# A hybrid decoder layer on eight cores: transposes moved from TensorE to SyncE's DMA queue, eight buffers for the first loads, weight blocks cut in quarters

## The reference, cut to what matters

```python
a = rmsnorm(h, g_mix)
q, k, v, r, alow, u, vg = split_cols(a @ w_in, IN_SIZES)
# gated linear attention, S_t = diag(exp(log_a_t)) S_{t-1} + k_t^T v_t ; o_t = q_t S_t, per head
o, s_new = gla_recurrence(q, k, v, log_sigmoid(alow @ w_a2 + b_a) / 16, s0)
o = rmsnorm(o, g_gla_norm) * silu(r)
# spatial gate in chunks of 128 positions
vn = layernorm(gelu(vg), g_gmlp_ln, b_gmlp_ln)
m = rmsnorm(chunk_spatial_gate(gelu(u), vn, w_s, b_s), g_gmlp_out)
h = h + concatenate([o, m], axis=-1) @ w_out
f = rmsnorm(h, g_ffn)
gate, up = split_cols(f @ w_ffn_in, (5632, 5632))
h = h + (silu(gate) * up) @ w_ffn_out
h = h + rmsnorm(p_l @ w_ple, g_ple) * sigmoid(rmsnorm(h, g_ple_gate) @ w_ple_gate)
y = rmsnorm(h, g_final)
```

## Time and profile before

| | us |
|---|---|
| median of 3 runs | 1927.8 (1926.95 to 2220.32) |
| the profiled execution | 1927.42 |
| its span, slowest core | 1926.0 (cores: 1919.8 to 1926.0) |
| TensorE busy with matmuls | 1799.0 |
| VectorE, ScalarE, GpSimd busy | 785.6, 530.1, 117.6 |

### The profile page before, as it was taken

How to read it: one execution, slowest core, us unless ns; L and a number is a source line. 1 busy time by engine, 2 the same in 40 slices (tenths; PEclk the granted TensorE clock), 3 DMA queues, 4 the chain that set the end, 5 groups by cost and what they waited for, 6 DMA issues and landing times.

```text
span 1926.0 us, 27025 instructions; the slowest of 8 cores (1919.8 to 1926.0 us)
## 1 busy us (share of the span) xinstructions
PE 1799.0 (93%) x10124; PEld 953.7 (50%) x10124; DVE 785.6 (41%) x1242; ACT 530.1 (28%) x899; POOL 117.6 (6%) x133
## 2 busy tenths in 40 slices
PE   3888879989999999999999999999999999998996
PEld 2345434444444456655555656565656555544442
DVE  5545512461274351141515151515151515186666
ACT  4545413463471141000000000010100000026786
POOL 1001112120110000000000000000000000000000
PEclk9889989999999999999999999999999999999998
DMA  8930283506645524424242424334342434244212
GB/s 223 214 112 34 99 186 110 110 12 137 142 98 154 84 46 91 88 45 88 44 88 44 88 50 83 61 71 72 61 87 50 84 58 77 50 104 90 70 49 110
DMA packets 26198, 171.56 MB, mean 89 GB/s; under 512 B 3156, under 2 KB 4564, under 8 KB 13144
## 3 DMA queue, kind: packets, MB, share of 16 engines
q0 software_dynamic: 13248, 108.94, 32.3%
q1 hardware_dynamic: 12816, 60.90, 9.0%
q10 hardware_dynamic: 8, 0.01, 0.0%
HBM read 259.90 MB, written 18.87 MB: 145 GB/s over the span
## 4 chain that ended last, share of the span: by engine, by line
PE 80%; DMA 6%; DVE 5%; ACT 5%; issue 4%; DVEq 0%; ACTq 0%; POOL 0%; POOLq 0%; SPq 0%
PE pf L483 79%; ACT arena L445 3%; DVE arena L455 2%; DVE arena L463 1%; DMA arena<-xp 1%; DMA arena<-w_pg 1%; PE pb L493 1%; DMA arena<-xm 1%; DMA sso<-arena 1%; DMA arena<-st 1%; ACT L476 1%; ACT L445 1%; DMA arena<-w_al 1%; DVE arena L727 1%; DVE arena L452 0%
## 5 line engine op out<-in xcount | busy, mean ns | idle before, releaser
L483 PE MATMUL pf<-arena 128*128 128x384 bf16 (+4 forms) x9352 | 1754.2, 352 | 78.3 <-ACT arena L449 16.4
L483 PEld LDWEIGHTS pf<-arena 128*128 128x128 bf16 (+1 forms) x9352 | 904.3, 99 | 905.9 <-issue 117.6
L455 DVE TENSOR_TENSOR arena<-pf,arena 128x512 f32<-128x512 f32 (+3 forms) x641 | 419.4, 661 | 844.6 <-PE pf L483 774.9
L445 ACT ACTIVATE arena<-pf 128x384 bf16<-128x384 f32 (+4 forms) x310 | 159.2, 526 | 997.7 <-PE pf L483 980.6
L445 ACT ACTIVATE arena<-arena 128x512 f32<-128x512 f32 (+7 forms) x131 | 144.3, 1108 | 149.9 <-DVE arena L455 86.7
L455 DVE TENSOR_TENSOR arena<-arena 128x512 f32<-128x512 f32 (+6 forms) x139 | 101.1, 744 | 57.3 <-ACT arena L445 23.6
L463 DVE SCALAR_TENSOR_TENSOR arena<-arena 128x2048 bf16<-128x2048 f32 (+3 forms) x67 | 118.2, 1775 | 5.0 <-DVE arena L478 1.2
L449 ACT COPY arena<-pb 128x1024 bf16<-128x1024 bf16 x71 | 69.8, 1001 | 94.9 <-PE pb L493 94.8
L493 PE MATMUL pb<-arena 128*128 128x128 bf16 x772 | 60.3, 231 | 33.6 <-ACT arena L449 9.5
L184 POOL DMA_DIRECT2D arena<-w_f x55 | 29.0, 528 | 1018.7 <-PE pf L483 1015.8
L459 POOL TENSOR_TENSOR arena<-arena 128x1024 f32<-128x1024 f32 x30 | 66.3, 2213 | 356.3 <-ACT arena L449 226.4
(11 more groups left out here) (27 smaller groups left out, 88.8 us busy)
## 6 DMA issues: line engine op xcount, KB each, us to landing
arena<-w_f POOLq DMA_DIRECT2D x44, 1024.0 KB, 10.1
arena<-w_f POOLq DMA_DIRECT2D x11, 2048.0 KB, 14.7
arena<-xm SPq DMA_DIRECT2D x18, 1024.0 KB, 8.0
arena<-w_tok POOLq DMA_DIRECT2D x8, 2048.0 KB, 18.4
y<-arena SPq DMA_DIRECT2D x18, 512.0 KB, 2.8
arena<-xp SPq DMA_DIRECT2D x8, 1024.0 KB, 13.5
arena<-st SPq DMA_DIRECT2D x16, 512.0 KB, 4.6
sso<-arena SPq DMA_DIRECT2D x16, 512.0 KB, 2.9
```

The source lines that it names most:

```text
L445: S.op("act", lambda: nc.scalar.activation(out=out, in_=in_, func=func, **kw), reads=reads, writes=writes, cost=c_act(n, ptr) + (0.17 if " ...
L455: S.op("dve", lambda: nc.vector.tensor_tensor(out=out, in0=a, in1=b, op=op), reads=reads, writes=writes, cost=c_dve(n, rate))
L483: ins = nc.tensor.matmul(o, lhsT=l, rhs=r, start=st, stop=sp_)
```

## The change

1. `S.dmaT` is new: a DMA on SP with `transpose=True`, from SBUF to SBUF. It takes the place of the TensorE transposes and of the copies out of `pb` for the keys (`ktok`, eight of 128x512 to 128x4x128), the attention result (`catO`, nine of 128x1024), the spatial gate's result (`catM`, nine), the feed-forward norm (18) and the gate's norm (18): 54 of 128x1024 and eight of 128x512. The first norms of `xp` and `xm`, the keys of the first half and the sample keys stay on TensorE.
2. The eight `xp` tiles get eight buffers: two in `MI`, and two each in `RING[3]`, `RING[1]` and `RING[2]`. The `xm` loads cycle through the first four of them (before: two). So `w_tok` for the values waits for the buffers in rings 1 and 2, and `w_q` for the last use of those in ring 3. `g_mix` is loaded by one DMA on SP; a square root of a small tile (`pcol`) is issued at the start.
3. The weight blocks lie in HBM in quarters (`w_f1` in halves): 2048 values of a partition are contiguous, where 8192 were (`w_f1`: 4096). One DMA still loads the whole block.
4. The scheduler's constants: `DMA_RATE` 3.2e5 instead of 3.9e5, and `DMA_T`, 4.0, as the cost of a transposing DMA.

```diff
-DMA_RATE = 3.9e5
+DMA_RATE = 3.2e5
+DMA_T = 4.0
...
+    def dmaT(self, out, in_, reads=(), writes=(), boost=0.0):
+        nb = 2.0 * in_.shape[0] * in_.shape[1]
+        prev = self._touch(list(reads) + list(writes))
+        self.pend.append(Op("dma", "sp", (out, in_, True), list(reads), list(writes), writes[0], DMA_T, prev, nb, boost + self.bst))
...
+        if len(o.fn) == 3:
+            self.eng[e].dma_start(out=o.fn[0], in_=o.fn[1], transpose=True).then_inc(kb.dsem, 16)
...
-    w_tok = din("w_tok", [8, 128, 16, 512])
+    w_tok = din("w_tok", [8, 4, 128, 2048])
...
-            S.dma("pool", t, src, writes=[b], key=ring_key[i], after=after)
+            S.dma("pool", t.rearrange("p (q k) n -> p q (k n)", q=4), src.rearrange("q p n -> p q n"), writes=[b],
+                  key=ring_key[i], after=after)
...
-        for i in range(4):
-            t_, r_ = (MI if i < 2 else RING[3]).T([128, D], F32)
+        for i in range(8):
+            t_, r_ = (MI, RING[3], RING[1], RING[2])[i // 2].T([128, D], F32)
...
-        for n_ in range(4):
-            px.append(xload(xp, porder[n_], 4))
+        for n_ in range(8):
+            px.append(xload(xp, porder[n_], 8, 5000.0 - n_))
...
-        Wk, BWk = win_ch(0, w_k, "k", [[px[2][1]], [px[2][1]], [px[3][1]], [px[3][1]]])
+        Wk, BWk = win_ch(0, w_k, "k", [[px[1][1]], [px[3][1]], [px[5][1]], [px[6][1]]])
...
-                x_, Bx_ = xload(xm, t, 2)
+                x_, Bx_ = xload(xm, t, 4)
...
-                for tp in range(2):
-                    t0 = 4 * g + 2 * tp
-                    trans_to([kT[:, c, (t0 + u) * 128:(t0 + u + 1) * 128] for u in range(2) for c in range(4)], BkT[g],
-                             ktok[:, t0:t0 + 2, :], [Bktok[t0 // 2]], "act", 1024)
+                for c in range(4):
+                    S.dmaT(ktok[:, 4 * g:4 * g + 4, c * 128:(c + 1) * 128], kT[:, c, c0:c0 + n], [BkT[g][c]], [Bktok[4 * g + c]])
...
-            trans_to([on[i][:, j * 128:(j + 1) * 128] for j in range(8)], [Bon[i]], catO[:, t, :, :], [BcatO[t]], "act", 1024)
+            S.dmaT(catO[:, t, :, :], on[i], [Bon[i]], [BcatO[t]])
...
-            trans_to([mn[mi][:, j * 128:(j + 1) * 128] for j in range(8)], [Bmn[mi]], catM[:, t, :, :], [BcatM[t]] + Bgu[t], "act", 1024)
+            S.dmaT(catM[:, t, :, :], mn[mi], [Bmn[mi]], [BcatM[t]] + Bgu[t])
...
-            norm_p2(xf[t % 2], [Bxf[t % 2]], lambda hf: (catO if hf == 0 else catM)[:, t, :, :], Bf[t])
+            for hf in range(2):
+                S.dmaT((catO, catM)[hf][:, t, :, :], xf[t % 2][:, hf * 1024:(hf + 1) * 1024], [Bxf[t % 2]], [Bf[t][hf]])
...
-            norm_p2(xg[t % 2], [Bxg[t % 2]], lambda hf: (catO if hf == 0 else catM)[:, t, :, :], Bf[t], ("act", "act"))
+            for hf in range(2):
+                S.dmaT((catO, catM)[hf][:, t, :, :], xg[t % 2][:, hf * 1024:(hf + 1) * 1024], [Bxg[t % 2]], [Bf[t][hf]])
```

More of the change, by code:

```diff
@@ L183, in _emit @@
         kb.dcnt += 16
-        self.eng[e].dma_start(out=o.fn[0], in_=o.fn[1]).then_inc(kb.dsem, 16)
+        if len(o.fn) == 3:
+            self.eng[e].dma_start(out=o.fn[0], in_=o.fn[1], transpose=True).then_inc(kb.dsem, 16)
+        else:
+            self.eng[e].dma_start(out=o.fn[0], in_=o.fn[1]).then_inc(kb.dsem, 16)
         self._commit((kb.dsem, kb.dcnt), o.reads, o.writes)
@@ L389, in build_nc @@
     g_gout = din("g_gout", [1024])
-    w_out = din("w_out", [4, 128, 16, 512])
+    w_out = din("w_out", [4, 4, 128, 2048])
     g_ffn = din("g_ffn", [D])
-    w_f1 = din("w_f1", [2 * NFB, 2, 128, 16, 256])
-    w_f2 = din("w_f2", [NFB, 128, 4, D])
-    w_ple = din("w_ple", [128, 2, D])
+    w_f1 = din("w_f1", [2 * NFB, 2, 2, 128, 2048])
+    w_f2 = din("w_f2", [NFB, 4, 128, D])
+    w_ple = din("w_ple", [2, 128, D])
     g_ple = din("g_ple", [D])
     g_pg = din("g_pg", [D])
-    w_pg = din("w_pg", [4, 128, 16, 512])
+    w_pg = din("w_pg", [4, 4, 128, 2048])
     g_fin = din("g_fin", [D])
@@ L606, in build_nc @@
         dset(cm[:, :, 8:10], Bcm[3], 0.0)
+        S.op("dve", lambda: nc.vector.memset(pcol, 1.0), writes=[Bpcol], cost=0.1, boost=5000.0)
         def norm_p1(src, Bsrc, gain, Bg, xn, Bxn, ss, Bss):
@@ L733, in build_nc @@
         porder = [4, 5, 6, 7, 0, 1, 2, 3]
-        for c in range(4):
-            S.dma("act", grow[32 * c:32 * c + 1, :], g_mix[c * 512:(c + 1) * 512].unsqueeze(0), writes=[Bgrow[c]], boost=5000.0 - c)
+        S.dma("sp", grow[0:128:32, :], g_mix.rearrange("(c n) -> c n", c=4), writes=[Bgrow], boost=9000.0)
         px = []
-        for n_ in range(4):
-            px.append(xload(xp, porder[n_], 4))
+        for n_ in range(8):
+            px.append(xload(xp, porder[n_], 8, 5000.0 - n_))
             if n_ == 1:
-                S.dma("sp", wa2b, w_a2b, writes=Bwa2)
-        Wk, BWk = win_ch(0, w_k, "k", [[px[2][1]], [px[2][1]], [px[3][1]], [px[3][1]]])
+                S.dma("sp", wa2b, w_a2b, writes=Bwa2, boost=4998.5)
+        S.op("act", lambda: nc.scalar.activation(out=pcol[:, 0:1], in_=pcol[:, 0:1], func=AF.Sqrt, bias=EPS, scale=1.0), reads=[Bpcol],
+             writes=[Bpcol], cost=1.5, boost=5000.0)
+        Wk, BWk = win_ch(0, w_k, "k", [[px[1][1]], [px[3][1]], [px[5][1]], [px[6][1]]])
         bg_ = [nextpf() for _ in range(4)]
         MM([(bg_[c][0][:], onerow[32 * c:32 * c + 1, :], grow[32 * c:32 * c + 1, :], True, True) for c in range(4)],
-           [Bonerow] + Bgrow, [x[1] for x in bg_], 2.0)
+           [Bonerow, Bgrow], [x[1] for x in bg_], 2.0)
         for c in range(4):
@@ L795, in build_nc @@
             prev_norm(n_)
-        for n_ in range(4, 8):
-            px.append(xload(xp, porder[n_], 4))
         d1 = prev_decay(1)
@@ L856, in build_nc @@
         ktok, r_ = MI.T([128, 8, 512], BF16)
-        Bktok = S.bufs(4, "ktok", [part(r_, 2048 * i, 2048) for i in range(4)])
+        Bktok = S.bufs(8, "ktok", [r_] * 8)
         kTs, r_ = MI.T([128, 4, 128], BF16)
@@ L1488 @@
     blocks = lambda w, n: np.ascontiguousarray(w.reshape(16, 128, -1, n).transpose(2, 1, 0, 3))
+    quart = lambda w: np.ascontiguousarray(w.reshape(4, 4, 128, -1, 512).transpose(3, 0, 2, 1, 4)).reshape(-1, 4, 128, 2048)
     wa2b = np.zeros((128, 128), np.float32)
@@ L1492 @@
         wa2b[32 * c + 16] = f(b_a).reshape(512)[c * 128:(c + 1) * 128]
-    wf1 = f(w_ffn_in).reshape(16, 128, 2, 2 * NFB, 256)
+    wf1 = f(w_ffn_in).reshape(2, 8, 128, 2, 2 * NFB, 256)
     shared = {
         "g_mix": f(g_mix).reshape(D), "w_q": blocks(win[:, 0:512], 128), "w_k": blocks(win[:, 512:1024], 128),
-        "w_tok": blocks(np.concatenate([win[:, 1024:3072], win[:, 3088:5136]], axis=1), 512),
+        "w_tok": quart(np.concatenate([win[:, 1024:3072], win[:, 3088:5136]], axis=1)),
         "w_al": np.ascontiguousarray(win[:, 3072:3088].reshape(16, 128, 16).transpose(1, 0, 2)),
@@ L1500 @@
         "b_sT": np.ascontiguousarray(np.concatenate([bsT, np.tile(bsT[0:8], (16, 1))], axis=1)),
-        "g_gout": f(g_gmlp_out).reshape(1024), "w_out": blocks(f(w_out).reshape(D, D), 512), "g_ffn": f(g_ffn).reshape(D),
-        "w_f1": np.ascontiguousarray(wf1.transpose(3, 2, 1, 0, 4)),
-        "w_f2": np.ascontiguousarray(f(w_ffn_out).reshape(NFB, 4, 128, D).transpose(0, 2, 1, 3)),
-        "w_ple": np.ascontiguousarray(f(w_ple).reshape(2, 128, D).transpose(1, 0, 2)),
-        "g_ple": f(g_ple).reshape(D), "g_pg": f(g_ple_gate).reshape(D), "w_pg": blocks(f(w_ple_gate).reshape(D, D), 512),
+        "g_gout": f(g_gmlp_out).reshape(1024), "w_out": quart(f(w_out).reshape(D, D)), "g_ffn": f(g_ffn).reshape(D),
+        "w_f1": np.ascontiguousarray(wf1.transpose(4, 3, 0, 2, 1, 5)).reshape(2 * NFB, 2, 2, 128, 2048),
+        "w_f2": f(w_ffn_out).reshape(NFB, 4, 128, D),
+        "w_ple": f(w_ple).reshape(2, 128, D),
+        "g_ple": f(g_ple).reshape(D), "g_pg": f(g_ple_gate).reshape(D), "w_pg": quart(f(w_ple_gate).reshape(D, D)),
         "g_fin": f(g_final).reshape(D),
```

32 lines of the change are left out of this document (17 added, 15 removed).

## The result

The changed kernel takes 1954.4 us (median of 4, 1953.9 to 1956.2), the kernel before 1927.4: a ratio of 1.0143 (95% interval 1.0123 to 1.0163). The prediction was 1882 us, with a range to 1922.

What follows compares the result with a forecast made beforehand. TensorE, busy 1799.0 of 1926.0 us, was taken as the bound, with 127 us idle. Terms -15 - 10 - 10 - 6.5 - 5.5 + 2 = -45 us on 1927.4 gave 1882 us; forecast 1870 to 1897, wider range 1864 to 1922.

Steps and rivals of the forecast that it cites:

- term 4: Feed-forward norm: nine transpose groups off a never-idle TensorE, minus 8.0, plus a 1.5 us first-SiLU wait: minus 6.5 us.
- Term 5: Gate's norm at the end: fewer transposes and copies, less work behind the last w_pg wait: minus 5.5 us.
- Term 3: Mixer: transposes for keys, catO and catM leave TensorE and their copies leave ScalarE: minus 10 us.
- Term 6: SP's queue: state loads, stores and h loads stand behind 62 new entries waiting on VectorE: plus 2 us.
- Term 2: Stall at 266 us: quartered rows shorten the state's store and load beside w_tok to 6.4 us each: minus 10 us.
- Term 1: The start: eight xp buffers land tiles earlier, four xm buffers cut waits for xm: minus 15 us.
- Rival A: Transposing DMA is slow, at the xg and xf cycles and first SiLU, so the kernel ends slower; chance 0.11.

Runs made afterwards that it cites:

- loads_only: The changed kernel with all transposing DMAs put back on TensorE, its buffers, quartered weight blocks and scheduler constants kept: 1900.2 us, ratio 0.9857 to the kernel before.
- The start's part alone: The changed kernel with all transposes back on TensorE and weight blocks in whole rows again, leaving the start's buffers, g_mix DMA and DMA_RATE: 1915.8 us, ratio 0.9935.
- plain_copy: The changed kernel with each of the 62 transposing DMAs replaced by an ordinary DMA of the same bytes, not transposed: 1919.5 us, ratio 0.9956.
- quiet_mixer: loads_only with transposing DMAs only for catO of tiles 0 to 5 and catM of tiles 0 to 3: 1902.7 us.
- fnorm_held: loads_only with the feed-forward norm alone transposed by DMA and the first two f2 blocks held until the last of these landed: 1895.6 us, ratio 0.9818.
- hold_loads: The changed kernel with the weight blocks that loaded beside transposing DMAs (u, w_tok, w_out, f2, w_pg) made to wait for them: 1927.4 us.
- transposes_only: The kernel before with the transposing DMAs in all five places and nothing else changed: 1999 us, ratio 1.0358.

## Why the prediction was wrong, step by step

**The step that failed** is the price of a transposing DMA in term 4, 4 us and 5 for a pair, where those in the chain took 17.5 to 30.1 us: "a lower bound ... is the store of 512 KB ..., 2.9 us; an upper one the same store beside weight blocks, 15.7 ... I take a value near the lower row". Term 5 used the same price, and terms 3 and 6 put nothing for a late one. Both rows belong to DMAs of 8 packets an engine. I scaled by bytes. Term 2 of the same prediction counted packets, each waiting for one of the other queue, and the trace of before has about as many of each where both queues are busy (257 to 260 us: 22 packets of q0, 26 of q1). With 66 packets an engine and the 0.38 us that term 2 gives a 4 KB packet, that same model gives some 29 us. The number of packets was in no row of before; but then 15.7 was no upper bound.

**Term 1** (-15) and **term 2** (-10): right together, -27 measured in loads_only for the -25. The eighth square starts at 40.0 us (41 forecast), u_gen at 88.1 (94). The start's part alone gave 12. The 5 us for the waits on xm came, but from the quarters, which term 1 had not counted there. In term 2 the mechanism is the one described; the transfer took 13.3 and not 6.4 us, probably because three of SP's transfers stood in line, and still 8.8 of 12.9 us of the wait went. In the changed kernel itself, with the keys' DMAs on the same queue, 8.5 us of that wait are left. The rule of the Trainium skill that I had weighed (DMA: Bandwidth & Descriptors, "Queues, rings and completion order": an engine changes queue between packets, and a packet typically holds 9 to 17 descriptors) would have made it zero. The traces have one packet for each contiguous piece, 29376 for 13248, and turns of one to one at every size; the measurement decides.

**Term 3** (-10): +23. TensorE's two long waits behind late DMAs are 12.9 and 14.8 us. Even without the collision it was worth nothing: 0.5 us in plain_copy, and no gain in quiet_mixer, where the waits for VectorE took back what the transposes gave. "About half lies in stretches that wait" was too little, and no run shows the 2 us for ScalarE's copies.

**Term 4** (-6.5): +14 with the collision, -9.3 without it (fnorm_held; -8.0 forecast for the transposes). The one place where TensorE never idled paid in full, as argued; TensorE's wait ahead of `ffn1` was 20.3 us for the 1.5 forecast, and 2.5 when the f2 blocks were held.

**Term 5** (-5.5): +16. The place named in the bound, two xg buffers and a pair P that outlasts VectorE's cycle, is where the changed kernel waits: ScalarE 21.9 us for xg. But that isn't the whole of it. plain_copy costs the same 16 us, and hold_loads 15 with no DMA there over 6.6 us. Term 4 had counted a wait of the first SiLU for the last tile's DMA; the same wait at this end, of the first sigmoids, term 5 put at nothing (17.6 us of TensorE in the changed kernel, part of it the late DMA ahead of it; 12.6 in hold_loads). How the 16 us divide between the collision, that wait and the load of `g_ple` behind the DMAs stays open: no run takes them apart.

**Term 6** (+2): about 4 in the sample loop of plain_copy (u blocks issued at 324.4 us, 320.3 in loads_only), nothing there in the changed kernel. In transposes_only it holds the largest single loss, TensorE's wait of 35.0 us. How the store came to be held up by a DMA behind it in the queue stays open.

Rival A (0.11) had the right places and the right signs, but took the DMA to be slow in itself; it isn't, with 3.2 us alone. What I held against it, a DMA share of 0.42 and 0.38, was an average over stretches whose loads come in bursts (0.87 from 716 to 736 us).
